# A two-layer hybrid encoder: q and k heads turned by a block transpose and a way through DRAM

## What is computed

```python
# layer 0
h = xn @ w_in
qa, ka, va, qb, kb, vb = split_heads(...)           # 8, 8, 8, 8, 2, 2 heads
oa = neighbourhood_attention(rms_norm(qa, a_qn), rms_norm(ka, a_kn), va, a_rpb)
qb = axial_rope(rms_norm(qb, b_qn), rows, cols)
kb = axial_rope(rms_norm(kb, b_kn), rows, cols)
ob = dense_gqa(qb, kb, vb)
x = x + concat(oa, ob) @ w_out
# layer 1
qc, kc, vc, qd, kd, vd = split_heads(...)           # 12, 4, 4, 12, 4, 4 heads
oc = window_gqa_sink(partial_rope(rms_norm(qc, c_qn), pos), partial_rope(rms_norm(kc, c_kn), pos), vc, c_sink)
od = dilated_attention(partial_rope(rms_norm(qd, d_qn), pos), partial_rope(rms_norm(kd, d_kn), pos), vd)
x = x + concat(oc, od) @ w_out
# after each
x = x + (silu(xn @ w_gate) * (xn @ w_up)) @ w_down
```

## Time and profile before

| what | value |
|---|---|
| median of 3 runs | 2149.07 us (2148.85 to 2149.70) |
| the profiled execution | 2148.37 us |
| its span, first to last instruction | 2146.6 us |
| TensorE busy | 2129.5 us |
| VectorE busy | 1380.5 us |
| ScalarE busy | 1001.7 us |
| GpSimd busy | 65.8 us |
| DMA | 399.32 MB, 186 GB/s |

### The profile page before, as it was taken

One profiled execution on the slowest core, in us unless ns is written; L12 is line 12 of the kernel. 1 busy time (PEld: TensorE's weight loads), 2 busy tenths in 40 slices (PEclk: granted clock), 3 DMA queues, 4 the chain that ended last, 5 costly groups with the idle time before them and its releaser, 6 DMA issues.

```text
span 2146.6 us, 28247 instructions
## 1 busy us (share of the span) xinstructions
PE 2129.5 (99%) x9540; PEld 1760.2 (82%) x9540; DVE 1380.5 (64%) x1807; ACT 1001.7 (47%) x1270; POOL 65.8 (3%) x55
## 2 busy tenths in 40 slices
PE   8999999999999999999999999999999999999999
PEld 7888888888888888888888778888888888888887
DVE  5755587676666766666666666786676666765443
ACT  6555555444444444444455556454444444444443
POOL 0000010000000000000011010000000000000000
PEclk9999999999999999999999999999999999999999
DMA  8545556666666665555665453466666666656654
GB/s 275 167 147 172 172 176 196 195 183 191 204 195 182 190 204 185 186 190 193 210 192 176 147 158 118 157 199 194 194 183 191 203 195 183 189 189 203 215 201 141
DMA packets 207805, 399.32 MB, mean 186 GB/s; under 512 B 13312, under 2 KB 13568, under 8 KB 207744
## 3 DMA queue, kind: packets, MB, share of 16 engines
q1 hardware_dynamic: 205296, 394.30, 59.4%
q10 hardware_dynamic: 2448, 4.21, 0.6%
HBM read 396.37 MB, written 2.10 MB: 186 GB/s over the span
## 4 chain that ended last, share of the span: by engine, by line
PE 96%; DVE 2%; ACT 1%; issue 0%; POOL 0%; DMA 0%; SPq 0%; ACTq 0%; DVEq 0%
PE psum L411 31%; PE psum L414 31%; PE psum L412 31%; PE psum L501 2%; PE psum L431 1%; PE psum L479 1%; ACT w_hi L578 1%; DVE w_lo L836 1%; DVE turn_sb L882 0%; POOL head_rstd L1156 0%; PE psum L499 0%; DMA x_res<-in_x 0%; ACT xt_hi L621 0%; DVE xt_lo L894 0%; DVE stage L976 0%
## 5 line engine op out<-in xcount | busy, mean ns | idle before, releaser
L836 DVE TENSOR_TENSOR w_lo<-w_raw,w_hi 128x1024 fp32r<-128x1024 f32 x760 | 908.5, 1202 | 625.8 <-ACT w_hi L578 620.4
L578 ACT ACTIVATE w_hi<-w_raw 128x1024 fp32r<-128x1024 f32 x760 | 786.3, 1041 | 937.0 <-PE psum L414 925.1
L411 PE MATMUL psum<-w_hi,xt_hi 128*128 128x512 f32 x2016 | 795.6, 395 | 3.8 <-DVE xt_lo L894 3.6
L414 PE MATMUL psum<-w_hi,xt_lo 128*128 128x512 f32 x2016 | 785.5, 390 | 0.0
L412 PE MATMUL psum<-w_lo,xt_hi 128*128 128x512 f32 x2016 | 784.8, 389 | 0.0
L411 PEld LDWEIGHTS psum<-w_hi,xt_hi 128*128 128x128 f32 x2016 | 378.8, 188 | 83.4 <-DVE xt_lo L894 4.8
L414 PEld LDWEIGHTS psum<-w_hi,xt_lo 128*128 128x128 f32 x2016 | 378.6, 188 | 79.7
L412 PEld LDWEIGHTS psum<-w_lo,xt_hi 128*128 128x128 f32 x2016 | 378.9, 188 | 77.8
L411 PE MATMUL psum<-w_hi,ht_hi 128*128 128x512 f32 x960 | 376.1, 392 | 0.0
L414 PE MATMUL psum<-w_hi,ht_lo 128*128 128x512 f32 x960 | 373.7, 389 | 0.0
L412 PE MATMUL psum<-w_lo,ht_hi 128*128 128x512 f32 x960 | 373.6, 389 | 0.0
(11 more groups left out here) (98 smaller groups left out, 606.7 us busy)
## 6 DMA issues: line engine op xcount, KB each, us to landing
w_raw<-in_w_gate SPq DMA_DIRECT2D x176, 512.0 KB, 3.7
w_raw<-in_w_up SPq DMA_DIRECT2D x176, 512.0 KB, 3.8
w_raw<-in_w_down SPq DMA_DIRECT2D x160, 512.0 KB, 4.2
w_raw<-in_cd_w_in SPq DMA_DIRECT2D x80, 512.0 KB, 3.8
w_raw<-in_ab_w_in SPq DMA_DIRECT2D x72, 512.0 KB, 3.7
w_raw<-in_ab_w_out SPq DMA_DIRECT2D x32, 512.0 KB, 3.6
w_raw<-in_cd_w_out SPq DMA_DIRECT2D x32, 512.0 KB, 3.6
w_raw<-in_w_down SPq DMA_DIRECT2D x32, 256.0 KB, 2.6
```

Source lines behind the costliest of these rows:

```text
L411: nc.tensor.matmul(acc, hi[:, chunk, ts], w_hi[:, slot, c, :], start=first and c == 0, stop=False)
L414: mm = nc.tensor.matmul(acc, lo[:, chunk, ts], w_hi[:, slot, c, :], start=False, stop=end)
L578: nc.scalar.activation(w_hi[:, slot, 0:n, :], w_raw[:, slot, 0:n, :], ACT.Copy).then_inc(hi_ready, 1)
L836: nc.vector.tensor_tensor(w_lo[:, slot, 0:n, :], w_raw[:, slot, 0:n, :], w_hi[:, slot, 0:n, :].bitcast(F32), ALU.subtract).then_inc(lo_rea ...
```

## The change

The heads of q and k tiles are no longer turned by TensorE. After normalisation and rotation VectorE turns the 32x32 blocks within `stage` into `turn_sb` in one instruction of 128x1024 (`blocks`; two smaller ones for kv_b). SP stores `turn_sb` to a DRAM tensor (`block_dram`), waits, and reads it back in four DMAs, one for each block column, which puts the blocks at their partitions. k_b, k_c and k_d land in their tiles straight away; q lands in `land_sb` and is copied by ScalarE to `qt_*`; k_a lands in `kt_a` and is scaled there by the product of the q and k gains. The transposes of the probabilities stay on TensorE, with one PSUM bank in place of two.

The layout of the turned heads changes: queries are [tile, token half, head, 128], keys are [tile, a, token half, head, 32], and TensorE reads a key head as 8 runs of 32 elements.

The sum of squares, its power and the normalisation are done for each token half in turn. Items start 3 to 5 ticks later. The output projection is written out unit by unit (`OUT_UNITS`): tiles 0 and 1 alternate in groups of four units, tile 1 in the second pair of accumulators, and attention may fill all 16 units. As those accumulators are the first score banks, the last 4 items of layer 0 and the last 8 of layer 1 use two banks outside them. `residual_lo` of the last tile of a phase comes after the split k = LEAD + 3, ahead of `mean_square`. The turn of output tile 0 goes to `land_sb` in place of `turn_sb`.

```diff
-AB_ITEMS = ([("b", h, 22 + 2 * h, 27 + 2 * h, 29 + 2 * h) for h in range(8)]
-            + [("a", h, t, t + 4, t + 6) for h, t in enumerate((45, 47, 49, 51, 68, 69, 70, 71))])
-CD_ITEMS = ([("d", s, 37 + 4 * s, 42 + 4 * s, 80 + s) for s in range(4)]
-            + [("c", h, *ticks) for h, ticks in enumerate(
-                [(61, 65, 67), (63, 67, 69), (65, 69, 71), (67, 71, 73), (69, 73, 75), (71, 76, 77), (73, 77, 78),
-                 (74, 78, 79), (76, 80, 82), (77, 81, 83), (78, 82, 84), (79, 83, 85)])])
+AB_ITEMS = ([("b", h, 25 + 2 * h, 30 + 2 * h, 32 + 2 * h) for h in range(8)]
+            + [("a", h, t, t + 4, t + 6) for h, t in enumerate((48, 50, 52, 54, 72, 73, 74, 75))])
+CD_ITEMS = ([("d", s, 41 + 4 * s, 46 + 4 * s, 82 + s) for s in range(4)]
+            + [("c", h, t, t + 4, t + (6 if h < 4 else 5)) for h, t in enumerate(
+                (65, 67, 69, 71, 73, 74, 75, 76, 81, 82, 83, 84))])
...
+OUT_UNITS = [(n, k) for half in range(2) for n in range(2) for k in range(4 * half, 4 * half + 4)]
+OUT_UNITS += [(n, k) for n in range(2, XT) for k in range(KU)]
+OUT_END = [max(i for i, (tile, _) in enumerate(OUT_UNITS) if tile == n) for n in range(XT)]
+PAIR_UNITS = 2 * KU
...
-            self.banks.append([0, 1, 2] if kind == "d" else [n % 3])
+            late = n - len(items) + (4 if layer == 0 else 8)
+            self.banks.append([0, 1, 2] if kind == "d" else [n % 3] if late < 0 else [2 + late % 2 * 2])
...
+        def keys(kind, h):
+
+            kt = {"a": kt_a, "b": kt_b, "c": kt_c, "d": kt_d}[kind]
+            return kt[:, h // 4, :, :, h % 4, :].rearrange("p a t i -> p t a i")
...
+            def move_qk(layer, v):
+
+                m = mixers[layer]
+                for q, p in enumerate(m.qk_tiles):
+                    _, kind, h0 = m.tiles[p]
+                    run = TOK * 32 * (2 if kind == "kv_b" else 4)
+                    at = m.qk_tick(p, 2) + RING + LEAD + 1
+                    if v == at:
+                        sp.wait_ge(qk_blocks, m.qk0 + q + 1)
+                        sp.dma_start(block_dram[:, :, 0:run], turn_sb[:, :, 0:run]).then_inc(blocks_out, 16)
+                    if v == at + 1:
+                        sp.wait_ge(blocks_out, 16 * (m.qk0 + q + 1))
+                        if kind[0] == "q" and m.finish_rank[p]:
+                            sp.wait_ge(qk_ready, m.finish_rank[p])
+                        dst = land_sb[:] if kind[0] == "q" else keys_tensor(kind)[:, h0 // 4]
+                        dst = dst.rearrange("p a t c i -> p a (t c i)")
+                        for b in range(4):
+                            src = block_dram[:, b, 0:run].rearrange("(a j) x -> j a x", a=4)
+                            sp.dma_start(dst[32 * b:32 * b + 32], src).then_inc(qk_landed, 16)
...
+                        move_qk(layer, KU * p + k)
                         load(u, k % RING, w_in[layer], UC * k, UC, slice(col * N, col * N + N), first=u < RING)
...
-                        wait_t_free(f)
+                        pe.wait_ge(t_read[0], XT + f)
...
-                        wait_read(pe, m.fill["qk", p, 0], m.fill["qk", p, 1])
+                        pe.wait_ge(qk_ready, m.finish_rank[p] + 1)
...
-                                mm = nc.tensor.matmul(dst, qt[:, qh, tok * P:tok * P + P], kt[:, kh, :],
+                                mm = nc.tensor.matmul(dst, query(kind, qh, tok), keys(kind, kh),
...
+                    if t == m.qk_tick(p, 8 if kind[-1] != "a" else 7) and p in m.finish_rank:
+                        act.wait_ge(qk_landed, 64 * (m.qk0 + q + 1))
+                        if kind != "k_a":
+                            dst = query_tile(kind, h0).rearrange("p t c (a i) -> p (t c) a i", a=4)
+                            src = land_sb[:].rearrange("p a t c i -> p (t c) a i")
+                            nc.scalar.activation(dst, src, ACT.Copy).then_inc(qk_ready, 1)
+                            continue
...
+                        nc.scalar.activation(tile, tile, ACT.Copy, scale=gain_qk[:]).then_inc(qk_ready, 1)
...
+            def blocks(layer, q, kind):
+
+                m = mixers[layer]
+                dve.wait_ge(qk_normed, m.qk0 + q + 1)
+                if m.qk0 + q:
+                    dve.wait_ge(qk_landed, 64 * (m.qk0 + q))
...
+                    src = stage[2 if kind in ("q_a", "k_a") else 0]
+                    dst = turn_sb[:].rearrange("p b (g i) -> p g b i", g=TOK * 4)
+                    ins = nc.vector.transpose(dst, src[:].rearrange("p t (c b j) -> p (t c) b j", c=4, b=4))
+                ins.then_inc(qk_blocks, 1)
...
-                            if half == 0 and k == LEAD + 4:
-                                if first:
-                                    residual_lo(layer, "out", XT - 1)
-                                else:
-                                    hidden_lo(layer, i - 1)
+                            if half == 0 and k == LEAD + 4 and not first:
+                                hidden_lo(layer, i - 1)
                             if first and half == 0 and k == LEAD + 3:
+                                residual_lo(layer, "out", XT - 1)
                                 mean_square(2 * layer + 1)
```

309 lines of the change are left out of this document (153 added, 156 removed).

## The result

The changed kernel takes 2153.84 us (median; 2153.32 to 2156.85) against 2148.84 (2147.97 to 2149.70) for the kernel before: ratio 1.0027, 95% interval 1.0018 to 1.0036. Forecast were 2132.3 us, 16.8 less. It is 5 us slower, so the sign was wrong too. The profiled execution took 2155.74 us, its span is 2153.9, against 2146.6 before: 7.3 more.

A forecast was written before the change was run, and what follows sets the result against it. TensorE, busy 2129.5 of 2146.6 us, was taken as the bound. Terms 12.6 + 5.0 + 0.2 - 1.0 = 16.8 us took 2149.07 to 2132.3 us; range 2129.5 to 2143.5.

The forecast's parts named there:

- Transposes off TensorE: In TensorE's stream, head transposes of 14 q/k tiles and kv_b go, none of their time hidden: 12.6 us gained.
- Waits that go: TensorE's waits for stage (0.9 us), three for xt_lo (3.6 in all) and one for probs (0.5) go: 5.0 us gained.
- The exchange in the scores: Late attention items: a 1.3 us wait for probs goes, 1.1 us comes at tick 75's scores: 0.2 us gained.
- VectorE's block transpose: Each q/k tile adds 1.24 us on VectorE; an earlier GpSimd power cancels it with the halved steps, so nothing moves.
- rival 4: TensorE reads the keys' runs of 32 elements at half rate in score matmuls: 2166 us; chance 0.03.
- The store and the reads: On SP's queue, store 3.5 us, reads 3.8; q_b's load 1.9 us late, TensorE not stalled; 1 us allowed in all.
- B + 9.9: Landing of the load of T+11 behind the reads, in us after B, the end of a tile's block transposes on VectorE.
- E(T+2): End of unit T+2, T being the unit number at which a q/k tile's 8 units have ended.
- Rival 1: Cover of the store-and-read round trip too thin: 4 to 11 us on top, 2136 to 2143; chance 0.22.
- Rival 3: Store and what waits at SP make it slower, 2151, from 17 us between blocks and landed weights; chance 0.07.
- Rival 2: Ticks pile up on VectorE in units 73 to 89, with 1 us waits in ten or so: 2143 to 2149; chance 0.10.
- Output projection: With tiles 0 and 1 interleaved, attention has 16 units of cover instead of 8; no wait expected there.

The follow-up runs named there:

- e3: Kernel before with only residual_lo of a phase's last tile moved ahead of the split LEAD + 4: 2144.54 us, ratio 0.9982.
- e1: Kernel before plus VectorE's block transposes into turn_sb, which nothing reads; TensorE still turns the heads: 2151.69 us, ratio 1.0014.
- e7: Changed kernel with store and reads of the q tiles and k_a carrying a quarter of the bytes: 2144.43 us, ratio 0.9978.
- e9: Changed kernel with the four reads of each q/k tile behind one more weight load on SP's queue: 2150.40 us, ratio 1.0008.
- e2: e1 plus the store and four reads on SP's queue, into a tile that nothing reads: 2155.57 us, ratio 1.0034.
- e6: Changed kernel with the store and four reads of each q/k tile issued by GpSimd in place of SP: 2167.62 us, ratio 1.0088.
- e5: Changed kernel with every head of b one unit later: 2151.65 us, ratio 1.0013.
- e14: e13 with layer 1's softmax of head d 3 one tick earlier and head c 0 one tick later: 2146.22 us, ratio 0.9983.
- e10: Changed kernel with residual_lo (the xt_lo work) of output tiles 0 and 1 left out in both layers: 2148.28 us.
- e12: Changed kernel with the edits of e5, e9 and e11 together: 2149.15 us, ratio 1.0004.
- e4: Changed kernel with the residual work of output tile 1 two units later: 2161.91 us, ratio 1.0061.
- e8: e4 with output tile 1's xt_lo behind tile 2's residual add: 2158.33 us, ratio 1.0043.
- e11: Changed kernel with output tile 1's xt_lo made by GpSimd (a multiply and a subtract) in place of VectorE: 2158.42 us, ratio 1.0045.
- e13: Changed kernel with the edits of e5 and e9 together: 2150.05 us, ratio 1.0004.

## Why the prediction was wrong

**Transposes off TensorE: right.** Forecast 12.6 us, measured some 12.0 by the stall sum.

**Waits that go: right, and more.** Forecast 5.0; 7.6 us of stalls went, 4.5 of them for xt_lo. e3 has that edit alone at -3.9. The wait of half a microsecond at layer 1's unit 42 did not go wholly (0.8 to 0.45). The exchange in the scores came as forecast: unit 68's 1.3 us of waiting is gone, and some 0.7 came at the scores of tick 75.

**VectorE's block transpose: price right, conclusion wrong.** Forms of the changed kernel (xcount | busy us, mean ns):
```profile
L994 DVE STREAM_TRANSPOSE turn_sb<-stage 128x1024 f32<-128x1024 f32 x14 | 17.4, 1246 | 0.5
...
L1197 POOL TENSOR_TENSOR head_rstd<-head_eps,minus_half 128x4 f32<-128x4 f32 x28 | 31.4, 1123 | 2.3
```
1246 ns, where I had 1.24 us. But a power over 4 columns takes 1.12 and not 1.01, VectorE still waits 0.9 us for it, now between the two halves, and the chain does not end where it did. "So nothing moves here" was read from one tile of q_b; e1 puts 3.3 us on it, most of it at a unit that already stalled in the kernel before and where the slack was therefore none. In the changed kernel, with its moved ticks, that unit (68) has no stall, so this price is not a term of its 5 us. The score matmuls (380 ns) are as they were: rival 4 was rightly small.

**The store and the reads: the landing right, the consequence missed.** Landing of the load behind the reads: forecast B + 9.9, measured B + 11.0 in the tile shown. B itself lies at E(T+2) + 6.9 there, where I had 3.8. A part of that was a slip: q_b's 6.4 less the 1.5 of the shorter rotation is 4.9, not 3.8. The rest is the wait between the halves and a start at E(T+2) + 1.1, which was 1.4 in the kernel before and should have become 0.2. The two together put the landing at E(T+2) + 17.9, 3.5 us later than ScalarE wants it, and it waited 3.35. The real error is the sentence that the load is 1.9 us late for q_b and for the others not, and that TensorE "doesn't feel it". It weighed the late w_hi against its own unit alone. On ScalarE the square of the next tile stands behind that w_hi, so the next chain, the next store and the next w_lo are late too, and the load behind the reads, which I took at 4.5 us (B + 5.4 to B + 9.9), lands after 6.4. e7 prices the bytes at 9.4 us, e9 gets 3.4 by order alone, e2 has the DMAs at 3.9 without the other changes. Rival 1, late q and k, hardly occurred: TensorE waited 1.2 us in all for a finished q. Rival 3 had the sign and the place (a q/k tile's store and reads on SP), but not the mechanism: it asked for 17 us and the landing is at 11.0; and in e6, with SP freed, the stalls stay.

**Ticks of the attention: not checked where it mattered.** I worked through ticks 74 and 75 and allowed nothing elsewhere. The shift by 3 put a row maximum on tick 26 of layer 0, and the one by 4 the softmax of the last d and the row maximum of the first c on 58 and 66 of layer 1, each the tick of a q chain. Rival 2 named this kind and looked at units 73 to 89. e5 and e14 price these three places at 2.2 and 3.8 us.

**Output projection: the part that I costed at nothing.** The sentence "attention has 16 units of cover instead of 8" looks at attention alone. The other side is that VectorE's residual work of two tiles now falls into 12 units: 12 w_lo of 1.23, 8 turns of 1.78, two adds of 1.29 and two xt_lo of 1.67 are 34.9 us against TensorE's 32.6. All but the add and xt_lo stand in the earlier trace rows, so it could have been added up. (Instructions that follow each other directly overlap a little: the timeline has VectorE at work for some 34.4 us of it.) Its stalls are 7.8 us, and e10 gets 5.6 of the time back.

By these runs: -12.0 and -7.6 are what the change gives; the new stalls are about 9 us of stores and reads beside the loads, 6 of three badly placed softmax steps and 8 of VectorE at the output tiles. These single prices were measured in differing surroundings and overlap (e12), and with the rest, some 4 us in units of under 2 us each, they make the 27 only roughly. Layer 0's unit 30 kept 0.8 to 1.9 us in all orders of the reads and ticks; only fewer bytes (e7) removed it. Unit 59 stands at 2.2 us in some executions and at 3.8 in others with the same wait; the difference is the clock, next section but one. Why the clock falls behind one such wait and not behind another stays open.

## What to carry to other kernels

When an engine at 99% is relieved, add up each other engine's work over the stretch in which the change puts it, not over the kernel: VectorE at 65% was over its capacity for 12 units. Follow a late step to everything queued behind it on its engine, above all to what starts the next turn of the same loop. And when items are shifted in a hand-written order, check each new tick against the ticks that are already full.

## What was not expected of the hardware

A store of 512 KB into DRAM lands in 2.7 us when the queue is drained, less than I took (3.5); four reads of 128 KB to 32 partitions each take 3.6 (up to 4.3) issued by SP, where each costs its queue 0.43 us, and 5.7 us issued by GpSimd. A weight load sent out behind them landed after 6.4 us and not 3.8.
A single wait of TensorE of 1.85 us can bring the granted clock down, and the same wait can leave it up. TensorE waits 1.85 us for probs at layer 1's unit 59 in the changed kernel and in all experiments on it but e14. Busy time and clock of the 3.5 us behind it, in the changed kernel and in e10:
```profile
1248.50:1252.00 3.50, 3.50 (x18) 2.88 (x17) 3.46 (x7) 1.05 (x2) 0.00 (x0) 1.00 0.51 141
...
1243.00:1246.50 3.50, 3.50 (x10) 2.73 (x9) 3.43 (x8) 0.52 (x1) 0.00 (x0) 0.51 0.52 152
```
TensorE gets through 18 matmuls in the first and 10 in the second, 0.43 us apart in place of 0.23; that is the 1.6 us between unit 59's 2.2 and 3.8. In e4, e5, e6, e7, e10 and e12 the clock fell there, in the changed kernel, e8, e9, e11 and e13 it did not. Nor did it behind a wait of 3.0 us at layer 0's unit 32 in e10, where it did in the changed kernel. Behind the longest waits, in e4, it was 0.80 over 17 us.

GpSimd's multiply of 128x256 takes 0.93 us in one place and 2.94 in the next (e12, two instructions of the same form, then VectorE's work at that time; spans on GpSimd are rough):
```profile
312.27 0.93 POOL L1214 TENSOR_SCALAR stage<-turn_sb,gain_x 128x256 f32<-128x256 f32 x1 [12.69 <-ACT xt_hi L645]
...
314.01 2.94 POOL L1214 TENSOR_SCALAR stage<-turn_sb,gain_x 128x256 f32<-128x256 f32 x1
...
311.15 1.23 DVE L857 TENSOR_TENSOR w_lo<-w_raw,w_hi 128x1024 fp32r<-128x1024 f32 x1
313.85 3.73 DVE L857 TENSOR_TENSOR w_lo<-w_raw,w_hi 128x1024 fp32r<-128x1024 f32 x3 [1.47 <-ACT w_hi L602]
```
VectorE stood idle during nearly all of the short one and ran three w_lo back to back during the long one. Layer 1 and e11 have the same pattern.

The Trainium skill ("SBUF — State Buffer", Who interferes with whom) says that a VectorE instruction with two inputs in SBUF and a GpSimd instruction that reads SBUF cannot run together: the one that starts first makes the other wait until it is done. VectorE's w_lo is such a one, at 1.2 us, and the 2.0 us that the second multiply takes longer agree with it; the third multiply, at 318.16 us, ran beside the residual add, which has one input in PSUM, and took 0.92.

Landings scatter, and with a thin cover the scatter becomes time. In e13's profiled execution ScalarE waited 1.8 us for a q tile, and TensorE lost 3.9 us at unit 64 (2.3 of standing still and 1.6 at the lower clock behind it); in e14, with the same order in that layer, 0.4:
```profile
ACT qt_a L716 <- DMA land_sb<-block_dram: 1.8, 1, 1.8
```
